# A transformer layer on one core: part of its down projections as seven products in place of eight

## The reference, cut to what matters

```
def swiglu(x, w_gate, w_up, w_down):
    return (jax.nn.silu(x @ w_gate) * (x @ w_up)) @ w_down

f = swiglu(rmsnorm(h, g_ffn1_pre[i]), w_ffn1_gate[i], w_ffn1_up[i], w_ffn1_down[i])
h = h + 0.5 * rmsnorm(f, g_ffn1_post[i])
```

## Time and profile before

| | |
|---|---|
| median of three runs | 1890.99 us |
| lowest, highest | 1890.77, 1891.41 us |
| span of the profiled execution, first to last instruction | 1889.1 us |
| around the span, to the median | 1.9 us |
| TensorE busy (matmuls) | 1878.1 us, 99% |
| VectorE busy | 1080.5 us, 57% |
| ScalarE busy | 883.9 us, 47% |
| weights and others moved | 371.5 MB, mean 197 GB/s |

### The profile page before, as it was taken

How to read it: one execution, slowest core, us unless ns; L and a number is a source line. 1 busy time by engine, 2 the same in 40 slices (tenths; PEclk the granted TensorE clock), 3 DMA queues, 4 the chain that set the end, 5 groups by cost and what they waited for, 6 DMA issues and landing times.

```text
span 1889.1 us, 24728 instructions
## 1 busy us (share of the span) xinstructions
PE 1878.1 (99%) x8658; PEld 1550.4 (82%) x8658; DVE 1080.5 (57%) x1208; ACT 883.9 (47%) x1179; POOL 112.8 (6%) x162
## 2 busy tenths in 40 slices
PE   9999999999999999999999999999999999999998
PEld 7888888888888888888888888888888888888886
DVE  5555555455544446777896755555555454444565
ACT  6444444444444346555555644444444344344563
POOL 1000000000000001013551100000000000000010
PEclk9999999999999999999999999999999999999999
DMA  7666666666665655655556566666666666656554
GB/s 258 202 207 202 203 193 193 210 214 215 204 202 196 200 195 165 201 168 167 152 178 204 165 212 207 203 203 207 202 193 193 202 229 198 201 192 207 191 190 145
DMA packets 214115, 371.54 MB, mean 197 GB/s; under 512 B 16592, under 2 KB 41632, under 8 KB 213664
## 3 DMA queue, kind: packets, MB, share of 16 engines
q1 hardware_dynamic: 213040, 367.20, 61.5%
q10 hardware_dynamic: 1008, 3.46, 0.5%
HBM read 358.01 MB, written 2.10 MB: 191 GB/s over the span
## 4 chain that ended last, share of the span: by engine, by line
PE 98%; DVE 1%; ACT 0%; issue 0%; POOL 0%; POOLq 0%; DVEq 0%; ACTq 0%
PE bank L533 31%; PE bank L535 31%; PE bank L534 31%; PE bank L846 1%; PE bank L637 1%; PE bank L875 1%; PE bank L857 1%; PE bank L693 0%; PE bank L821 0%; DVE w_rest L1340 0%; DVE x_rest L1355 0%; PE bank L606 0%; PE bank L596 0%; PE bank L610 0%; PE bank L683 0%; DVE resid L1364 0%
## 5 line engine op out<-in xcount | busy, mean ns | idle before, releaser
L1340 DVE TENSOR_TENSOR w_rest<-raw,w_high 128x1024 fp32r<-128x1024 f32 x654 | 801.6, 1228 | 700.2 <-ACT w_high L988 696.6
L988 ACT CAST w_high<-raw 128x1024 fp32r<-128x1024 f32 x654 | 685.0, 1050 | 895.6 <-PE bank L535 754.3
L533 PE MATMUL bank<-w_high,x_high 128*128 128x512 f32 (+1 forms) x1912 | 745.9, 390 | 0.7 <-DVE x_rest L1695 0.2
L535 PE MATMUL bank<-w_high,x_rest 128*128 128x512 f32 (+1 forms) x1912 | 741.1, 388 | 0.0
L534 PE MATMUL bank<-w_rest,x_high 128*128 128x512 f32 (+1 forms) x1912 | 740.6, 387 | 0.0
L533 PEld LDWEIGHTS bank<-w_high,x_high 128*128 128x128 f32 x1912 | 359.1, 188 | 74.5 <-issue 1.9
L535 PEld LDWEIGHTS bank<-w_high,x_rest 128*128 128x128 f32 x1912 | 359.0, 188 | 74.3
L534 PEld LDWEIGHTS bank<-w_rest,x_high 128*128 128x128 f32 x1912 | 359.2, 188 | 71.6
L533 PE MATMUL bank<-w_high,h_high 128*128 128x512 f32 x704 | 274.2, 390 | 0.0
L535 PE MATMUL bank<-w_high,h_rest 128*128 128x512 f32 x704 | 273.9, 389 | 0.0
L534 PE MATMUL bank<-w_rest,h_high 128*128 128x512 f32 x704 | 273.9, 389 | 0.0
(11 more groups left out here) (164 smaller groups left out, 735.9 us busy)
## 6 DMA issues: line engine op xcount, KB each, us to landing
raw<-in_w_ffn_up SPq DMA_DIRECT2D x176, 512.0 KB, 4.6
raw<-in_w_ffn_down SPq DMA_DIRECT2D x176, 512.0 KB, 4.3
raw<-in_w_ffn_gate SPq DMA_DIRECT2D x174, 512.0 KB, 4.5
raw<-in_w_qkv SPq DMA_DIRECT2D x68, 512.0 KB, 3.9
raw<-in_w_o SPq DMA_DIRECT2D x32, 512.0 KB, 4.1
raw<-in_w_ple_gate SPq DMA_DIRECT2D x32, 512.0 KB, 4.2
branch<-branch SPq DMA_DIRECT2D x320, 32.0 KB, 1.9
resid<-in_x SPq DMA_DIRECT2D x8, 256.0 KB, 6.6
```

The lines of the kernel that those rows point to most:

```text
L533: nc.tensor.matmul(o[:, 0:width], xh, wh, start=first and c == 0, stop=False)
L535: ins = nc.tensor.matmul(o[:, 0:width], xr, wh, start=False, stop=last and c == chunks - 1)
L988: nc.scalar.copy(slot(n, k)[0], raw[:, k]).then_inc(w_high_done, 1)
L1340: nc.vector.tensor_tensor(to_rest, raw[:, k], to_high.bitcast(F32), ALU.subtract).then_inc(w_rest_done, 1)
```

## The change

Columns are taken in pairs of blocks (`even`, `odd`), and a list `PAIR_ORDER` of 56 operations is gone through for each of the two pairs. 28 of them are slots as before ("plain", 12 matmuls). The other 28 are four groups of seven products with 6 matmuls each. A group covers 512 rows of w_down by 1024 columns, that is four slots B11, B12, B21, B22, and both tiles of tokens: the 2 x 2 x 2 block product that took eight half-slot products is done with seven (Strassen's scheme in Winograd's form). Its weight operands are B22, B21, B11 and four sums, which VectorE makes in place:

- sum1 = B11 + B12, sum3 = B12 + B22, sum2 = sum1 + B22, sum4 = sum2 + B21;
- B11 and B12 are loaded beside the ring, to two places in `branch` (`chain(j, 0)`, `chain(j, 1)`); B22 and B21 stay in the ring until sum2 and sum4 have been made.

Each weight operand, sums too, gets its high part from ScalarE and its rest from VectorE, as any slot does, in the same four buffers. The activations need four combinations for a group ("mixed"), made once in the first pair: `combine` (five operations on VectorE, three of them waited for), a copy on ScalarE and `combine_rest` on VectorE; both pairs use them from `x_high` and `x_rest`, which are free at that time. Three products (sum1, sum2, sum3) and the one shared first product (B11) accumulate over the groups in banks 4 to 7; `fix_odd` (six operations of 128 x 512) and `fix_even` (two) add them to the blocks near the end of a pair.

The order of a pair: six plain slots; group 0; three plain slots; group 1; three; group 2; three; group 3; three; six. A group is b22, b21, b11, sum1, sum3, sum2, one plain slot, sum4. `combine` for groups 1 to 3 stands seven operations before the group.

More of the change, by code:

```diff
@@ L67, in layer_program, with plains @@
     S_FFN1 = 0
+    GROUPS = 4
+    RING_KINDS = ("plain", "b22", "b21")
+    def plains(which, s0, s1):
+        return [("plain", which, s) for s in range(s0, s1)]
+    def group(i, inner):
+        return ([(kind, None, i) for kind in ("b22", "b21", "b11", "sum1", "sum3", "sum2")] + inner
+                + [("sum4", None, i)])
+    G0 = 2 * GROUPS
+    PAIR_ORDER = (plains(0, G0, G0 + 6) + group(0, plains(0, G0 + 6, G0 + 7)) + plains(0, G0 + 7, G0 + 10)
+                  + group(1, plains(1, G0, G0 + 1)) + plains(1, G0 + 1, G0 + 4)
+                  + group(2, plains(1, G0 + 4, G0 + 5)) + plains(1, G0 + 5, G0 + 8)
+                  + group(3, plains(0, G0 + 10, G0 + 11)) + plains(0, G0 + 11, FS) + plains(1, G0 + 8, FS))
+    PAIR_OPS = len(PAIR_ORDER)
+    RING_AT = [sum(kind in RING_KINDS for kind, _, _ in PAIR_ORDER[:t]) for t in range(PAIR_OPS + 1)]
+    PAIR_RING = RING_AT[PAIR_OPS]
+    PLACE = {item: t for t, item in enumerate(PAIR_ORDER)}
+    GROUP_AT = [PLACE["b22", None, i] for i in range(GROUPS)]
+    GROUP_END = [PLACE["sum4", None, i] for i in range(GROUPS)]
+    SUM_AT = {"sum1": 1, "sum3": 2, "sum2": 3, "sum4": 4}
+    COMBINE_AT = [0] + [at - 7 for at in GROUP_AT[1:]]
+    T_FIX, T_EVEN, T_ODD = GROUP_END[-1], GROUP_END[-1] + 3, PAIR_OPS - 1
+    assert PAIR_OPS % RING == 0 and PAIR_RING % RING == 0 and PAIR_ORDER[T_EVEN] == ("plain", 0, FS - 1)
+    LAG = (PAIR_OPS - PAIR_RING) * (NBD // 2)
     S_DOWN1 = S_FFN1 + 2 * KS * FB
-    S_QKV = S_DOWN1 + NBD * FS
+    S_QKV = S_DOWN1 + PAIR_OPS * (NBD // 2)
     TS = KS * TAIL // NB
@@ L106, in layer_program @@
     U_PLE = U_P + 1
-    S_TURN_P = 12
+    T_TURN_P = PLACE["plain", 1, FS - 5]
     UW = NB // BPB
@@ L333, in layer_program @@
         pair_bank, o_bank, head_bank = bank[6], bank[7], bank[4:6]
+        P_FIRST, P_SUM2, P_SUM1, P_SUM3 = bank[4:8]
+        MIXED_AT = {"sum1": 0, "sum2": 1, "sum3": 2, "b22": 3}
         def o_place(q):
@@ L421, in _ @@
             ffn(S_FFN2, w_ffn2_gate, w_ffn2_up, 1)
[L422 removed]
+            down(S_DOWN2, w_ffn2_down, g_ffn2_post, 1)
             for nb in range(NBD):
@@ L544, in use_slot, with use_last_slots @@
                 ins.then_inc(w_used, 1)
-            def use_last_slots(n, k, high, rest, chunk, pair, slots=2, first=False, after=None, between=None):
+            def use_last_slots(n, k, high, rest, chunk, pair, slots=2, first=False, after=None, between=None,
+                               go_on=False):
                 for t in range(T):
@@ L771, in down @@
                 last = 2 if f else LAST_DOWN
[L772 to L783, removed]
+                even, odd = acc[b0 % 2], acc[(b0 + 1) % 2]
@@ new lines, in fix_even, with out @@
+                def fix_even(j):
+                    first, left = fix_place(j)[:, 0, 0, :], fix_place(j)[:, 1, 0, :]
+                    dve.wait_ge(w_used, n0 + PAIR_OPS * j + T_EVEN + 1)
+                    nc.vector.tensor_tensor(even[0][:], even[0][:], first, ALU.add)
+                    nc.vector.tensor_tensor(even[1][:], even[1][:], left, ALU.subtract).then_inc(fixed_even, 1)
+                def out(nb):
+                    dve.wait_ge(row_landed[nb % 2], 16 * (2 * f + nb // 2 + 1))
+                    for t in range(T):
+                        dve.wait_ge(squared, Q[job] + T * nb + t + 1)
+                        ins = times_gain(nb, t)
+                    ins.then_inc(branch_ready, 1)
```

313 lines of the change are left out of this document (239 added, 74 removed).

## The result

The changed kernel takes 1905.45 us (median of four runs, 1901.45 to 1907.09) against 1891.0: ratio 1.0073, interval 1.0059 to 1.0088, so 11 to 17 us slower. The forecast was 1890.4 us, with a range of 1884 to 1900. The result is outside, on the side of a rival that had a chance of 0.09: b21 waits behind the two loads beside the ring.

The account below looks back on a forecast made before the run. TensorE, busy 99%, was taken to bound the kernel: 96 matmuls fewer save 21.8 us, VectorE's stalls return 10 x 1.06 + 6 x 1.76 us, net -0.6 from 1890.99, so 1890.4 us; range 1884 to 1900.

Parts of the forecast that it names:

- b21 waits behind the two loads beside the ring: Slower rival, SyncE's queue: loads over 1.65 us apart make b11 1.6 us late in 16 groups, +25 us, 1916; chance 0.09.
- the one on the loads: Group's loads, 0 at its first product on TensorE: b21 issued at -10.1, landing at -4.9; no cost, 1.3 us cover.
- The burst I read: Profile's loads after a held queue: first landed 3.7 us after issue, next 1.28 and 1.24 us apart, 334 GB/s.
- The lead of 1.34 us: Ring: VectorE's subtraction starts 1.34 us after TensorE starts operand n-3; b11's therefore at -1.38 before a group.
- eight steps and two detours: VectorE's queue from b11: eight steps of 1.135 us, two detours through ScalarE of 0.065 more; inner plain slot's subtraction at 7.83.
- the rival without overlap: Slower rival: VectorE's in-place additions followed only at their end, 1.23 us a step; +13 us, 1904; chance 0.07.
- a rule of the Trainium skill: VectorE's next operation can't start before the previous pipe is empty; the trace disagreed by 0.09 us for each operation.
- The stall of 1.06 us: TensorE waits at a group's inner plain slot, losing 1.06 of 1.36 us saved, in 10 groups: 10.6 us.
- Combine's 0.7 us: Groups 1 to 3 of first pairs: combine makes b11 0.7 us late, so the stall is 1.76 us in six groups.
- The fixes cost nothing: `fix_odd` ends at 18.5 us into group 3, TensorE asks at 21.4; `fix_even` stands among plain slots: no cost.
- the whole sum, -0.6 us: Whole kernel: 21.8 us saved on TensorE, 10.6 and 10.6 us lost to stalls, net -0.6; this case's chance 0.48.
- Group 0 of the first projection's first pair: Six plain slots absorb combine and its rest (3.9 us) before b11 is due, so only the 1.06 us stall remains.

Follow-up runs that it names:

- run 1: Changed kernel with SyncE issuing b21's load ahead of the loads of B11 and B12, not behind them: 1891.59 us, ratio 1.0002.
- run 6: run 1 with combine for groups 1 to 3 left out (one column to a scrap place, products on old data): 1887.38 us, ratio 0.9981.
- runs 1 and 2: First: see run 1. Second: changed kernel with the loads of B11 and B12 cut to 16 of 512 columns (stale sums): 1891.69 us, ratio 1.0003.
- run 3: Changed kernel with each group's four additions cut to one column in a scrap tile, products on unsummed data, loads' order unchanged: 1869.12 us, ratio 0.9884.
- run 9: run 8 with combine for groups 1 to 3 left out (one column to a scrap place, stale data): 1869.34 us, ratio 0.9885.
- run 8: Changed kernel with a group's order b22, b11, plain, sum1, b21, sum2, sum3, sum4: 1878.12 us, ratio 0.9932.
- run 4: Changed kernel with the loads of B11 and B12 for groups 1 to 3 issued by ScalarE on its own DMA queue: 1902.4 us, ratio 1.0060.
- run 10: Changed kernel with b21 moved behind sum1 in a group's order, and combine's five operations on GpSimd in place of VectorE: 1889.19 us, ratio 0.9990.
- run 5: Changed kernel with the load of B12 alone cut to 16 of 512 columns (sums with stale data): 1892.24 us, ratio 1.0009.

## Why the prediction was wrong

**The step that failed** is the one on the loads: "So b21 lands at -4.9, against a copy due at -5.2 and a last moment of -3.6 from which it would delay b11. No cost, 1.3 us of cover." Its time of issue was right (b21 at -10.1) in all of groups 1 to 3 but one. The landing was wrong. The sum behind the -4.9 starts with b22, issued at -12.3 and landed 3.65 us later as if alone, and adds 1.25 us for each of the three loads behind it, both from one burst. In group 2 above, a plain load had been issued 1.14 us ahead of b22; b22 landed 5.5 us after its issue (669.6), and b21 5.1 us after that (674.7), 1.7 us for each load. So b21 landed 8.2 us after its own issue where I had 5.2, and 1.8 us ahead of the group (674.7 against 676.5) where I had 4.9. In eleven of the twelve groups 1 to 3 it missed the last moment of -3.6 by 0.4 to 2.3 us, in the twelfth by 4.2. The burst I read was only four loads, issued within 1.7 us with the next one 4.4 us behind, and three landings are few; two of the later ones in the same row of rows 8, issued 1.3 us apart (466.6 and 467.9), landed 2.4 us apart. The same stretch showed 334 GB/s over 6 us, which is 1.57 us for a load of 512 KB: that row alone would have made the cover 0.3 us, not 1.3, and the case likely.

The rival that held this had the right mechanism, and a threshold (1.65 us for each load) close to the 1.7 of group 2, though it too left out that b22 would be late. Its price was too high, +25 us: it let b11 be 1.6 us late in all 16 groups. Three groups, the first of each second pair and of the second projection's first pair, had no late load. And in first pairs combine would have made b11 0.7 us late anyway: it was 0.7 to 1.8 us late there, and these six groups lost only 3.1 us beyond forecast, the six of the second pairs 12. What was measured for the loads is 13.9 us (run 1 against the changed kernel).

**What held.** The lead of 1.34 us behind TensorE's start of operation n-3: 627.84 against 629.22. The pace of VectorE: eight steps and two detours put the inner slot at +7.83, measured +7.86, so additions in place cost the same 1.135 us and the rival without overlap falls. Again an operation starts 1.14 us after one that lasts 1.23 (628.98 behind 627.84). The prediction had weighed a rule of the Trainium skill ("VectorE: DVE Perf Modes", The DRAIN you can't avoid) against this and read half of it: the same section adds that a next operation that is not held starts earlier, and the 1.14 us agree with that. The stall of 1.06 us: 1.0 to 1.1 in the three groups without a late load, and in ten groups of run 1. Combine's 0.7 us in each of six groups: 4.2 us in run 6. The fixes cost nothing; no first slot of an odd block waited. Without late loads the whole sum, -0.6 us, stands beside +0.5 and +0.6 measured in runs 1 and 2. Group 0 of the first projection's first pair, which I had called spared, lost 1.7 us in the changed kernel and 1.1 in run 1: its b21 too was late, landing at -3.0.

**What it comes to.** TensorE saved 21.8 us. In the changed kernel some 36 us were given back: about 18 to VectorE's queue with its work in this order (21.8 + 0.5 of run 1, less combine), 4.2 to combine, and 13.9 to b21's place in SyncE's queue. Seven products for eight are worth all of their 21.8 us (run 3, run 9) once no group asks VectorE for more than its lead; in the best complete version 12.9 us remain (run 8).

**Open.** Why b22 took 5.5 us behind one load and the next three landed 1.7 us apart, while the windows of that stretch show 258 to 331 GB/s, that is 1.6 to 2.0 us for 512 KB, wasn't taken apart. Nor why SyncE stood 3.57 us over the two issues at 639.54 and only 0.88 over those at 665.29 (3.32 on ScalarE's queue in run 4). The number of loads under way doesn't tell them apart: in both cases it was three, issued at the same distances.

## What to carry to other kernels

Where fewer matmuls shorten the time that an operand is used for, the lead of a ring, counted in operands, shrinks with it: walk through the queue of the engine that prepares operands, one operation after the other, from the last moment that the ring holds it back. If that engine then has no slack, each load in front of it needs a margin of its own. Count every load that is still under way when it is issued, those ahead of the burst too, and price them at the rate of a window or worse, never by the best spacing seen. Before leaving a saving for lost, move a long operation behind the one that makes extra work: here the order of a group's operations turned +14 us to -13, though moving b21's load alone had already brought +14 to +0.5.

## What the runs showed of the hardware that I had not expected

- GpSimd and VectorE on float32 tensors in SBUF slow each other: VectorE's 128 x 1024 operation takes 1.76 us in place of 1.22 beside 128 x 256 ones, 3.26 beside a 128 x 1024 one (run 10). GpSimd's own 128 x 1024 operation took 2.40 us when it started ahead of VectorE's and 3.24 when it started during one. The Trainium skill ("GPSIMD Engine Reference", Specifications) says that the two share SBUF interfaces and that a VectorE instruction with two SBUF inputs contends; the trace agrees, with these numbers.
- With the side loads on ScalarE's queue b21 was little sooner there (run 4: 1902.4 us, landings 5.9 to 8.4 us after issue). The Trainium skill ("Trainium Kernel Development and Optimization", Key Constraints) says that loads of all queues run on the same DMA engines and interleave, and that issuing from several engines saves only the time of issue; the trace agrees.
- One issue of a 512 KB load took 3.16 us on SyncE where the same issue in the next group took 0.47, and it delayed the loads behind it by 2.5 us (changed kernel, at 639.95).
- The four runs of the changed kernel spread over 5.6 us, the ten of run 1 over 0.9 and the ten of run 5, whose b21 lands about at the last moment, over 4.2: where loads land near their moment the time is less steady.
